# Modulation rows of the next layer beside the FFN: channel products and sums on GpSimd, the sum over partitions on PE with a column of ones

## The reference

```python
def modulation(cvec, w_mod, b_mod):
    m = jax.nn.silu(cvec) @ w_mod + b_mod          # w_mod: 1024 x 6144 per layer
    return jnp.split(m, 6, axis=-1)
...
xp = xp + p_g1 * op
xs = xs + s_g1 * os_
hp = modulate(rmsnorm(xp, norm2_g[i]), p_sh2, p_sc2)
hs = modulate(rmsnorm(xs, norm2_g[i]), s_sh2, s_sc2)
xp = xp + p_g2 * conv_ffn(hp, ffn_w_in[i], ffn_conv_w[i], ffn_conv_b[i], ffn_w_out[i])
```

## Time and profile before

| | us |
|---|---|
| median of 3 runs | 3141.87 (3138.94 to 3143.25) |
| the profiled execution's own time | 3137.11 |
| its span in the trace | 3135.3 |
| PE busy | 3047.7 (97%) |
| DVE busy | 2077.4 (66%) |
| ACT busy | 1081.2 (34%) |
| POOL busy | 403.5 (13%) |

### The profile page before, as it was taken

How to read it: one execution, slowest core, us unless ns; L and a number is a source line. 1 busy time by engine, 2 the same in 40 slices (tenths; PEclk the granted TensorE clock), 3 DMA queues, 4 the chain that set the end, 5 groups by cost and what they waited for, 6 DMA issues and landing times.

```text
span 3135.3 us, 55240 instructions
## 1 busy us (share of the span) xinstructions
PE 3047.7 (97%) x21634; PEld 2791.6 (89%) x21634; DVE 2077.4 (66%) x4004; ACT 1081.2 (34%) x2250; POOL 403.5 (13%) x392
## 2 busy tenths in 40 slices
PE   8999999999999999999999899999999889999999
PEld 6899999886699999998876699999998769999999
DVE  7766666777756666668657566666667775766665
ACT  3332222336623222224345432222233663422221
POOL 3000000133310000003237410000012231000000
PEclk9999999999999999999999999999999999999999
DMA  8533323110033332321200223233231002122211
GB/s 340 217 121 120 111 106 131 61 58 1 10 112 135 121 111 106 131 100 54 81 32 8 90 100 115 105 129 120 100 111 54 4 1 95 68 81 80 67 67 48
DMA packets 47202, 290.20 MB, mean 93 GB/s; under 512 B 4945, under 2 KB 11345, under 8 KB 13265
## 3 DMA queue, kind: packets, MB, share of 16 engines
q1 hardware_dynamic: 47058, 288.21, 25.4%
HBM read 283.98 MB, written 4.21 MB: 92 GB/s over the span
## 4 chain that ended last, share of the span: by engine, by line
PE 89%; DVE 5%; ACT 2%; DMA 2%; issue 1%; POOL 0%; SPq 0%; DVEq 0%; ACTq 0%
PE psA L2014 38%; PE psB L2014 24%; PE psA L2123 4%; PE psA L2124 3%; PE psA L2129 3%; PE psB L2031 2%; PE psB L741 2%; PE psA L811 2%; PE psA L2200 1%; DMA w_stage<-weights_dram 1%; PE psB L723 1%; PE psA L709 1%; PE psB L869 1%; DVE top L1623 1%; PE psA L2205 1%
## 5 line engine op out<-in xcount | busy, mean ns | idle before, releaser
L2014 PE MATMUL psA<-h_hi,w_hi 128*128 128x320 f32 (+1 forms) x2736 | 624.9, 310 | 2.6 <-ACT u_raw L2367 1.7
L2014 PE MATMUL psA<-h_lo,w_hi 128*128 128x320 f32 (+1 forms) x2720 | 620.3, 309 | 0.0
L2014 PE MATMUL psA<-h_hi,w_lo 128*128 128x320 f32 x2704 | 616.2, 309 | 0.0
L2554 DVE SCALAR_TENSOR_TENSOR xT<-psB,mod,xT 128x128 f32<-128x128 f32 x750 | 377.7, 546 | 221.7 <-PE psB L2014 221.7
L2014 PEld LDWEIGHTS psA<-h_hi,w_hi 128*128 128x128 f32 x2736 | 456.3, 188 | 4.2 <-ACT u_raw L2367 2.5
L2014 PEld LDWEIGHTS psA<-h_lo,w_hi 128*128 128x128 f32 x2720 | 455.1, 188 | 0.0
L2014 PEld LDWEIGHTS psA<-h_hi,w_lo 128*128 128x128 f32 x2704 | 452.0, 188 | 0.0
L2613 DVE TENSOR_SCALAR conv<-u_raw,vec_sb 128x642 f32<-128x642 f32 x176 | 108.3, 615 | 438.9 <-ACT u_raw L2367 438.9
L2431 DVE TENSOR_TENSOR w_lo<-w_stage,w_hi 128x512 fp32r<-128x512 f32 x496 | 353.0, 756 | 37.8 <-ACT w_hi L2282 37.7
L2014 PE MATMUL psB<-g_hi,wo_hi 128*128 128x320 f32 x1280 | 299.3, 315 | 0.1
L2014 PE MATMUL psB<-g_hi,wo_lo 128*128 128x320 f32 x1280 | 295.2, 312 | 0.0
(11 more groups left out here) (272 smaller groups left out, 4970.6 us busy)
## 6 DMA issues: line engine op xcount, KB each, us to landing
w_stage<-weights_dram SPq DMA_DIRECT2D x124, 1024.0 KB, 5.1
m_stage<-w_mod_dram SPq DMA_DIRECT2D x96, 1024.0 KB, 8.3
wo_stage<-w_out_dram SPq DMA_DIRECT2D x44, 1024.0 KB, 4.8
yT_dram<-xT SPq DMA_DIRECT2D x8, 322.0 KB, 2.2
xT<-xT_dram SPq DMA_DIRECT2D x1, 1544.0 KB, 9.8
xT<-xT_dram SPq DMA_DIRECT2D x1, 1032.0 KB, 6.3
w_stage<-weights_dram SPq DMA_DIRECT2D x2, 512.0 KB, 17.9
rope_raw<-rope_dram SPq DMA_DIRECT2D x3, 256.0 KB, 2.6
```

The source lines that it names most:

```text
L2014: ins = pe.matmul(o, wp, xp[:, a:b], start=first and n == 0, stop=last and n == 2)
L2554: ins = dve.scalar_tensor_tensor(out=xT[:, d, c:c + w], in0=tokens(ps, slot)[i], scalar=gate[:, d, i:i + 1], in1=xT[:, d, c:c + w], op0=AL ...
```

## The change

Nine of the 12 passes of each of the three layers that have a next one (passes 1 to 9, `POOL_PASSES`) are computed in another way. POOL takes the staged weights and multiplies each tile of 128 channels by the conditioning value of its partition, once for each of the two vectors (16 multiplications of 128x512 elements), and adds the eight products up in `mod_acc` (14 additions of 128x512). PE then sums over the 128 partitions with `pick`, a column of ones among 32: 4 matmuls of 128 columns per half. The transposes take 64 rows instead of 128 and stand behind `u_tile` 3 instead of ahead of it; the wait for `mod_rows` stays ahead of `u_tile` 3. DVE then adds 2 partial sums instead of 4. POOL's pass i waits for its two DMAs, for the norm ahead of the FFN, and until PE has taken `mod_acc` of pass i - 1. SP's load of the next pass waits for POOL's last addition (`s_macc`) instead of PE's matmuls. Passes 0, 10 and 11 stay as they were. One semaphore is given up for the new one: the mask's load now counts on `s_small`. In the diff the first `mod_added` is POOL's, the second PE's.

```diff
+POOL_PASSES = 9
...
                     if l < DEPTH - 1:
-                        sp.wait_ge(s_mraw, it * 2 + 2 * (MOD_PASSES * (l + 1) + 1))
+                        if pooled:
+                            sp.wait_ge(s_macc, it + POOL_PASSES * l)
+                        else:
+                            sp.wait_ge(s_mraw, it * 2 + 2 * (MOD_PASSES * (l + 1) + 1))
                         load_m(it + (MOD_PASSES * (l + 1) + 1), 0)
...
+            def mod_added(l, i):
+                for g in range(2):
+                    pool.wait_ge(s_m[0][g], i * 16 + 16 * (6 + MOD_PASSES * l + 1))
+                for k in range(KT):
+                    dst = mod_prod[k % 2] if k else mod_acc
+                    for c in range(2):
+                        w = m_stage[0][:, :, k, :]
+                        if k == 0 and c == 0:
+                            pool_own(pool.tensor_tensor(dst[c][:, :, :], w, cond[:, k, c:c + 1].unsqueeze(2)
+                                                        .to_broadcast([P, 2, 2 * P]), ALU.mult))
+                        else:
+                            pool_own(pool.tensor_scalar(dst[c][:, :, :], w, cond[:, k, c:c + 1], 1.0, ALU.mult, ALU.mult))
+                    for c in range(2 if k else 0):
+                        last = k == KT - 1 and c == 1
+                        pool.wait_ge(s_pown, pool_own.loop + (pool_own.n - (not last)))
+                        ins = pool.tensor_tensor(mod_acc[c][:, :, :], mod_acc[c][:, :, :], dst[c][:, :, :], ALU.add)
+                        if not last:
+                            pool_own(ins)
+                ins.then_inc(s_macc, 1)
...
+                if l < DEPTH - 1:
+                    pool.wait_ge(s_h, KT * (2 * l + 1))
+                    mod_added(l, 1)
...
+                    with pool.Fori(2, POOL_PASSES + 1) as i:
+                        pool.wait_ge(s_mraw, i * 2 + 2 * MOD_PASSES * (l + 1))
+                        mod_added(l, i)
...
+            def mod_added(l, it, g):
+                pe.wait_ge(s_macc, it + POOL_PASSES * l)
+                for b, out in enumerate(beside(g)):
+                    for c in range(2):
+                        q = slice(32 * (2 * b + c), 32 * (2 * b + c + 1))
+                        ins = pe.matmul(out[q, :], pick[:, c, :], mod_acc[c][:, g, b * P:(b + 1) * P], start=True, stop=True)
+                ins.then_inc(s_mraw, 1)
+
+            def mod_added_sum(l, it):
+                for i, out in enumerate(beside(0) + beside(1)):
+                    r = slice(i % 2 * DH, (i % 2 + 1) * DH)
+                    ins = pe.transpose(out[:, 0:DH], mod_rows[r, i, :], ident[r, r])
+                ins.then_inc(s_mod, 1)
...
-                                mod_ffn(l, it + 1, d % 2)
+                                mod_added(l, it + 1, d % 2)
...
                     if not first and l < DEPTH - 1:
-                        mod_ffn_sum(l, it)
+                        pe.wait_ge(s_mrows, it * 2 + (MOD_PASSES * (2 * l + 1) + 2))
                     u_tile(it, 3, first)
+                    if not first and l < DEPTH - 1:
+                        mod_added_sum(l, it)
```

More of the change, by code:

```diff
@@ L173, in program @@
         xs = [at(f"xs{i}", [P, COLS], F32, B_NORM + (3 + i) * C) for i in range(2)]
+        mod_acc = [at(f"mod_acc{i}", [P, 2, 2 * P], F32, B_NORM + i * 2048) for i in range(2)]
+        mod_prod = [[at(f"mod_prod{k}{i}", [P, 2, 2 * P], F32, B_NORM + 4096 + (2 * k + i) * 2048) for i in range(2)]
+                    for k in range(2)]
+        assert 6 * 2048 <= 5 * C
         g_hi_last = at("g_hi_last", [P, 2, TOK], F32R, B_NORM + 5 * C + 4 * (NT + 4) * P)
@@ L239, in program @@
         ones = const("ones", [P, P])
+        pick = const("pick", [P, 2, 32])
         sq_tok = const("sq_tok", [P, NT])
@@ L282, in program @@
         s_count = sem("inv_count_loaded")
-        s_mask = sem("mask_loaded")
+        s_macc = sem("mod_products_added")
         s_act = sem("act_steps")
@@ L1503, in qkv_dve @@
             if l == 3:
-                dve.wait_ge(s_mask, 16)
+                dve.wait_ge(s_small, 64)
                 own(dve.tensor_copy(mask_r[:, :, :], mask_raw[:, :, :]))
@@ L1890, in _ @@
                     if l == 3:
-                        sp.dma_start(mask_raw[:, :, :].rearrange("p a n -> p (a n)"), t["mask"]).then_inc(s_mask, 16)
+                        sp.dma_start(mask_raw[:, :, :].rearrange("p a n -> p (a n)"), t["mask"]).then_inc(s_small, 16)
                     if l == 2:
@@ L1929, in _, with ffn_loads @@
                 cf = FFN_CHUNK[l]
-                def ffn_loads(it, last):
+                def ffn_loads(it, last, pooled=False):
                     load_w(it + (cf + 2), 0)
@@ L2005, in _ @@
                 norm_pow(2 * l + 1)
+                if l < DEPTH - 1:
+                    pool.wait_ge(s_h, KT * (2 * l + 1))
+                    mod_added(l, 1)
+                    per = 4 * KT - 3
+                    own_before = pool_own.n
+                    with pool.Fori(2, POOL_PASSES + 1) as i:
+                        pool_own.loop = (i - 2) * per
+                        pool.wait_ge(s_mraw, i * 2 + 2 * MOD_PASSES * (l + 1))
+                        mod_added(l, i)
+                    assert pool_own.n - own_before == per
+                    pool_own.loop = 0
+                    pool_own.n = own_before + per * (POOL_PASSES - 1)
         @block.tensor
@@ L2562, in _ @@
             own(dve.memset(ones2[:, :], 1.0))
+            own(dve.memset(pick[:, :, :], 0.0))
+            own.wait()
+            for c in range(2):
+                own(dve.memset(pick[:, c, c:c + 1], 1.0))
             own(dve.memset(hits[:, :, :], 0.0))
@@ L2676, in ffn_iter @@
                     if l < DEPTH - 1 and not (first and l):
-                        mod_bias(l + 1, it, blocks[:, :, 0:8:7, :].rearrange("p a b (q j) -> p a b j q", q=4)[:, :, :, 0:2, :], it + (MOD_PASSES * (l + 1) + 1))
+                        n = 4 if first else 2
+                        mod_bias(l + 1, it, blocks[:, :, 0:8:7, 0:32 * n].rearrange("p a b (q j) -> p a b j q", q=n)[:, :, :, 0:2, :], it + (MOD_PASSES * (l + 1) + 1))
                     glo(it, 1)
```

4 lines of the change are left out of this document (2 added, 2 removed).

## The result

The changed kernel takes 3500.86 us (3493.5 to 3501.57) against 3140.4 us before in the same runs: ratio 1.1142, 95% interval 1.1128 to 1.1155, 11.4% slower. The forecast was 3425 with a range of 3235 to 3580. The profiled execution took 3501.17 with a span of 3499.4, 364 more than before.

A forecast was written before the change was run, and what follows sets the result against it. POOL, not PE, was to set the FFN's pace: a loop of 17.9 + 1.7 + 35.4 = 55.0 us, 9.8 over 45.2, gives 235 over 24 turns; with 50 for pass 1, 3422, so 3425 us, range 3235 to 3580.

The forecast's parts named there:

- the loop: FFN turn: PE takes a pass, DVE makes `wo_lo`, SP loads, POOL computes the next; 55.0 us forecast against 45.2 before.
- the clock: PE's granted clock falls after each stand ahead of d = 6, slowing tiles 6 and 7: 1.7 us per turn.
- the exchange: POOL and DVE working together: POOL's pass loses 55% of DVE's 11.8 us of two-input time, 6.5 us.
- POOL's pass alone: POOL's multiplications and additions for one pass, without DVE beside them: 28.9 us.
- from taking to landing: From PE's first modulation matmul to the next pass's weights landing, by way of `wo_lo` and SP: 17.9 us.
- The rival that POOL loses nothing: In the FFN loop the exchange costs POOL nothing: loop 46.8 us, kernel 3213, or 3254 with the clock loss; chance 14%.
- the faster kernel: In the FFN the whole POOL pass fits and only PE's saving is left: 3092 us, break-even pass 27.3; chance 6%.
- The straight line for an addition: POOL's 512-element addition, read between 0.454 us at 128 elements and 1.538 at 640: 1.267 us.
- PE's saving: PE's modulation halves go from 16 matmuls to 4: 0.8 us saved per half, 1.6 per pass.
- The rival that DVE falls behind: DVE's 17 instructions each wait a whole POOL instruction and tile 6 waits: 3624 us; chance of over 3560: 10%.
- the cover: DVE's own loss beside POOL's pass, at most 16 us, falls in time when PE waits for POOL anyway.

The follow-up runs named there:

- port: Small separate program, not the kernel: POOL's 30 instructions of a pass alone, then beside three kinds of DVE instructions; a pass takes 28.2 us alone, 39.3 beside two-input ones.
- two_tiles: Against the changed kernel, POOL does only two of eight channel tiles in passes 1 to 9, the other six left out: 3104.40 us, ratio 0.9894 to before.
- warm: The changed kernel with 32 matmuls that nobody reads ahead of PE's wait for POOL in passes 1 to 9: 3459.99 us, ratio 1.1024 to before.
- load_first: Against the changed kernel, SP issues the next pass's loads ahead of the wait for `wo_lo`: 3308.36 us, ratio 1.0535 to before.
- four_tiles: Against the changed kernel, POOL does only four of eight channel tiles in passes 1 to 9, the other half left out: 3190.93 us, ratio 1.0157 to before.

## Why the prediction came out as it did

The forecast named the loop as the bound, and the order of engines in it was right at each place. PE waits for POOL in all 27 passes; the DMA of `m_stage` is still issued right behind `wo_lo`; the clock is at 0.50 behind the wait; turns of 58.0 lie at the upper end of the 50 to 58 named, passes of 37.2 within the 33 to 38. The waits are 6.9 us in most turns and not about 10, since PE comes to tile 6 later than I took it: DVE's late additions to `xT`, and the low clock behind them, stand in the same turn. Moving the loads (193 us) and keeping PE busy (41 us) both acted on the time as parts of a loop do.

The time was 76 us over the forecast. The mechanism was right; the terms of the exchange and of the clock were too small:

| term of a turn | forecast | measured |
|---|---|---|
| POOL's pass alone | 28.9 | 28.2 (port) |
| what it loses to DVE | 6.5 | 9.0 (37.2 less 28.2) |
| from taking to landing, without the clock | 17.9 | 18.2 (4.6 in two_tiles, and 13.6) |
| the clock | 1.7 | 2.2 (6.8 less 4.6) |
| turn | 55.0 | 57.6 (58.0 over all 24) |

24 turns of 3.0 us more are 71, and the takings of pass 1, later by 57 in all instead of 50, give 7: 78 of the 79 us between the sum of 3422 and the profiled 3501.17. POOL's pass alone was put 0.7 too high, which hides a part of the error of the exchange; that is luck.

**The exchange.** I took 55% of DVE's two-input time of 11.8 us, 6.5, and left the tensor_scalars out, with 1.0 per turn named for them. The 9.0 measured are 76% of it. During the pass shown DVE does 17 instructions with two inputs and three tensor_scalars; with the prices of the small program, 17 x 0.46 + 3 x 0.24 = 8.5 us. The rival that POOL loses nothing is out: 39.3 against 28.2 in the small program. So is the faster kernel: POOL's pass alone, 28.2, is already over the 27.3 at which the prediction breaks even. The straight line for an addition was good: 1.24 apart against 1.267.

**The clock.** The 1.7 was read from a place where PE had stood part of the time and then worked; behind a wait of 7 us it is 2.2, and keeping PE busy (warm) gives 2.1 of it back.

**PE's saving** was put at 1.6 per turn, by the number of matmuls; two_tiles gives 45.2 - 43.9 = 1.3, three steps of the 0.43 above. That is most of the 0.3 by which the way from taking to landing came out longer.

**The rival that DVE falls behind** was priced as an alternative to the loop, at 3624. The experiments show that it is true beside it: with four tiles it alone is worth 3.9 us per turn, 3190.93 against 3101.42. In the changed kernel it hides in PE's wait for POOL, which is 6.9 us in most turns with it and would be longer without it. The forecast was right to leave it out of the sum, but its sentence that the cover holds was argued and not shown; if the loop is mended, as in load_first, the cover is gone and PE waits 78 us for `xT`. That and the longer pass (39.8 and more) are why mending the loop by itself gave 3308 and not 3150. How the 78 divides between DVE's slower instructions and the clock behind them was not tried in that version.

## What to carry to other kernels

An engine that is idle over a whole stage can still not take a piece of it, if the piece lies in a loop with one buffer: add up the work and the way there and back, and compare with the iteration, not with the idle time. Price what the other engine pays as well: float32 instructions with both inputs in SBUF, and tensor_scalar in SBUF, cost GpSimd and VectorE about 0.2 to 0.6 us each where they meet, so the place of GpSimd's work in VectorE's schedule can matter more than its amount (90 us here for the same 14 instructions). Where PE must wait, look at the granted clock behind the wait: it was 0.50 behind waits of 7 us in the changed kernel, and the way that runs at it counts if it is in the loop. And where matmuls go to several column groups of the array, price them by the fullest group.

## What the runs showed of the hardware that was not expected

Both engines lose when they meet, by about the same: +0.46 us on GpSimd and +0.45 on VectorE for a two-input instruction of 512 elements. I had taken it that one of them stands for the other's whole instruction.

A VectorE instruction with one operand in PSUM costs GpSimd nothing (28.3 against 28.2), and is not slowed itself.

A stop of PE of only 2.16 us (four_tiles) was followed by 3.2 us of matmuls at half their rate (0.54 us a pair instead of 0.29), so a small wait for VectorE cost another 1.6 us. It is not so behind every stop: in load_first a stop of 3.12 us ends at 1155.44 and the granted clock stays at 1.00, 4.5 us to the u tile; behind an equal stop that ends at 1254.91 it is 0.57 and 0.58 between 1256 and 1260, and the same way takes 6.0 us.

Matmuls of 128 columns that go to four groups of 32 columns of the array cost by the fullest group, as far as six versions show it: 16 in four equal groups and 14 with a fullest group of four take the same (5.87 and 5.83 us from taking to u tile), and so do 12 and 10 with a fullest group of three (5.43 and 5.41).
